# Down stage of a hybrid decoder trunk: where activations' high parts, the plain fills' reads, the last block's sums and the norm pieces stand in each engine's order

## The reference

```python
def hybrid_layer(x, p_i, ...):                  # x: 1 x 1024 tokens x 1024
    ...                                         # token mixing, not touched
    h = rmsnorm(x, norm_ffn)
    gu = h @ w_gate_up
    x = x + (jax.nn.silu(gu[..., :D_FF]) * gu[..., D_FF:]) @ w_down    # D_FF = 2816
    hp = rmsnorm(x, norm_ple)
    x = x + jax.nn.sigmoid(hp @ w_ple_gate) * (p_i @ w_ple_proj)
    return x

def reference(...):
    for i in range(DEPTH):                      # DEPTH = 2
        x = hybrid_layer(x, p[i], ...)
    return rmsnorm(x, norm_final)
```

## Time and profile before

| | us |
|---|---|
| median of 3 runs | 2526.24 |
| the 3 runs | 2511.62, 2527.43, 2526.24 |
| the profiled execution | 2511.84 |
| its span, first to last instruction | 2510.1 |
| PE busy | 2432.6 (97%) |
| DVE, ACT, POOL busy | 1538.7, 968.4, 1207.7 |
| mean granted clock of TensorE | 0.991 of full speed |

### The profile page before, as it was taken

One profiled execution on the slowest core, in us unless ns is written; L12 is line 12 of the kernel. 1 busy time (PEld: TensorE's weight loads), 2 busy tenths in 40 slices (PEclk: granted clock), 3 DMA queues, 4 the chain that ended last, 5 costly groups with the idle time before them and its releaser, 6 DMA issues. The chain is left out here.

```text
span 2510.1 us, 30190 instructions
## 1 busy us (share of the span) xinstructions
PE 2432.6 (97%) x11528; PEld 2000.1 (80%) x11528; DVE 1538.7 (61%) x1946; ACT 968.4 (39%) x1424; POOL 1207.7 (48%) x772
## 2 busy tenths in 40 slices
PE   7999999999999989899999999999999999989898
PEld 6888888888888877777878887888888888777776
DVE  7967855554554566575596778546544544856735
ACT  4324244433333334345333242334333333333453
POOL 3212112288878847772221121123888787577520
PEclk9999999999999999999999999999999999999999
DMA  4342222123333354322143322311332334435111
GB/s 165 103 97 68 73 82 81 59 82 99 105 98 112 105 180 143 125 93 68 38 154 98 78 60 61 101 59 59 99 115 84 114 107 137 167 113 164 51 46 72
DMA packets 108415, 245.92 MB, mean 98 GB/s; under 512 B 35688, under 2 KB 44136, under 8 KB 104432
## 3 DMA queue, kind: packets, MB, share of 16 engines
q1 hardware_dynamic: 60880, 126.90, 16.6%
q10 hardware_dynamic: 47392, 117.09, 13.8%
HBM read 179.43 MB, written 51.41 MB: 92 GB/s over the span
## 5 line engine op out<-in xcount | busy, mean ns | idle before, releaser
L2116 POOL TENSOR_TENSOR w_lo<-w_raw,w_hi 128x1024 fp32r<-128x1024 f32 x100 | 261.1, 2611 | 922.6 <-ACT w_hi L1556 922.4
L2164 PE MATMUL proj<-h_hi,w_hi 128*128 128x512 f32 x1376 | 545.4, 396 | 0.9 <-POOL w_lo L2116 0.9
L2166 PE MATMUL proj<-h_lo,w_hi 128*128 128x512 f32 x1376 | 536.1, 390 | 0.0
L2165 PE MATMUL proj<-h_hi,w_lo 128*128 128x512 f32 x1376 | 535.7, 389 | 0.0
L2123 POOL TENSOR_TENSOR w_lo<-w_raw,w_hi 128x512 fp32r<-128x512 f32 x180 | 261.2, 1452 | 181.5 <-ACT w_hi L1538 181.5
L2164 PEld LDWEIGHTS proj<-h_hi,w_hi 128*128 128x128 f32 x1376 | 258.4, 188 | 57.3 <-issue 3.1
L2166 PEld LDWEIGHTS proj<-h_lo,w_hi 128*128 128x128 f32 x1376 | 258.3, 188 | 54.4
L2165 PEld LDWEIGHTS proj<-h_hi,w_lo 128*128 128x128 f32 x1376 | 258.4, 188 | 53.7 <-issue 2.4
L2123 POOL TENSOR_TENSOR w_lo<-turns,w_hi 128x512 fp32r<-128x512 f32 x180 | 253.9, 1411 | 98.0 <-ACT w_hi L1538 97.9
L1538 ACT ACTIVATE w_hi<-w_raw 128x512 fp32r<-128x512 f32 x180 | 112.6, 629 | 296.7 <-PE aux L2228 92.9
L1538 ACT ACTIVATE w_hi<-turns 128x512 fp32r<-128x512 f32 x180 | 113.5, 630 | 248.9 <-PE proj L2228 99.1
(11 more groups left out here) (329 smaller groups left out, 5295.8 us busy)
## 6 DMA issues: line engine op xcount, KB each, us to landing
w_raw<-weights SPq DMA_DIRECT2D x160, 512.0 KB, 3.5
turns<-weights SPq DMA_DIRECT2D x60, 512.0 KB, 4.0
act_sums_spill<-rows ACTq DMA_DIRECT2D x20, 1024.0 KB, 6.8
h_whole<-act_sums_spill ACTq DMA_DIRECT2D x40, 512.0 KB, 4.1
act_sums_spill<-act ACTq DMA_DIRECT2D x20, 512.0 KB, 5.2
ffn_b_whole<-act_sums_spill ACTq DMA_DIRECT2D x20, 512.0 KB, 4.9
act_sums_spill<-act ACTq DMA_DIRECT2D x20, 256.0 KB, 4.4
ffn_bw_whole<-act_sums_spill ACTq DMA_DIRECT2D x10, 512.0 KB, 3.6
```

What stands on the lines that cost most here:

```text
L2116: g.tensor_tensor(wlo[:, slot, 0:n], w, whi[:, slot, 0:n].bitcast(F32), ALU.subtract).then_inc(weights_ready.sem, 1)
L2164: pe.matmul(out, wh, rhi, start=first, stop=False)
L2165: pe.matmul(out, wl, rhi, start=False, stop=False)
L2166: return pe.matmul(out, wh, rlo, start=False, stop=final)
```

## The change

Four orders are written differently; no arithmetic is added or removed.
1. On ACT, in the groups: `load_part` and `act_high` now stand ahead of `highs_ahead`.
2. On DVE, in the plain fills: the fills' adds come first, and the last block's two `finish_act` and its three sums stand between them; low parts 5 and 6 move into group 0.
3. On ACT, ahead of and in the plain fills: the first high part ahead of the last store of activations, the store of the sums behind the weight operands.
4. The norm's pieces: fewer of them in groups 8 and 9, 8 of the 16 squares move behind group 9 (ACT: between the reads of the projection's fills), and PE's `sums` from behind fill 9 to behind fill 15.

```diff
@@ vector
                     v.wait_ge(up_scaled.sem, up_scaled.at(L, 2 * b + 2))
-                    finish_act(L, NSTD + b, 1)
-                    finish_act(L, NSTD + b, 0)
-                    act_sums(L, b)
+                    if b < NBS - 1:
+                        finish_act(L, NSTD + b, 1)
+                        finish_act(L, NSTD + b, 0)
+                        act_sums(L, b)
@@ vector, ffn_down
                 for k in range(16):
                     add_fill(L, U_DN + k // 8, k % 8, k // 2, k % 2)
-                    if k % 2 and k < 14:
-                        act_low(L, NSTD + k // 2)
+                    if k in (0, 1):
+                        finish_act(L, FT - 1, 1 - k)
+                    if k in (3, 5, 7):
+                        if k == 3:
+                            for h in range(2):
+                                v.wait_ge(act_made.sem, act_made.at(L, 2 * FT))
+                        act_sum(L, 2 * DPARTS - 1, (k - 1) // 2)
+                    if k in (4, 6, 9, 11, 13):
+                        act_low(L, NSTD + (4, 6, 9, 11, 13).index(k))
...
                         down_add(L, g, i)
+                        if g == 0 and i in (0, 1):
+                            act_low(L, NSTD + 5 + i)
...
                         elif g == NDB - 1:
-                            if i == 0:
-                                ple_square(L, 5)
-                                ple_square(L, 6)
-                            if i == 1:
-                                ple_square(L, 7)
-                            if i == 2:
-                                ple_lows(L, 0, 2)
-                            if i == 3:
-                                ple_square(L, 8)
-                                ple_square(L, 9)
-                                ple_lows(L, 2, 4)
-                            if i == 4:
-                                ple_lows(L, 4, 6)
-                            if i == 5:
-                                ple_square(L, 10)
-                                ple_square(L, 11)
-                                ple_lows(L, 6, 7)
-                for j in range(12, 16):
+                            if i in (0, 1):
+                                ple_square(L, 4 + 2 * i)
+                                ple_square(L, 5 + 2 * i)
+                            elif i < 6:
+                                ple_lows(L, i - 2, i - 1)
+                ple_lows(L, 4, 16)
+                for j in range(8, 16):
                     ple_square(L, j)
-                ple_lows(L, 7, 16)
@@ scalar, ffn_down
-                store_block(L, NBS - 1)
-                for i in range(3):
+                act_high(L, NSTD)
+                store_acts(L, NBS - 1)
+                for i in (1, 2):
                     act_high(L, NSTD + i)
                 a.wait_ge(unit_done.sem, unit_done.at(L, U_DN + 1))
                 highs_ahead(L, 7 * NBS + 2)
                 highs_ahead(L, 7 * NBS + 3)
+                store_sums(L, NBS - 1)
                 for i in range(3, 7):
                     act_high(L, NSTD + i)
...
                         a.wait_ge(product_done.sem, product_done.at(L, k + 1))
-                        highs_ahead(L, k + 6)
                         if q < DPARTS - 1:
                             if not second:
                                 load_part(L, q + 1, i)
                             if (i >= 4) == (not second):
                                 act_high(L, NSTD + 7 * (q + 1) + (i + 3 if second else i - 4))
-                        elif not second:
+                        highs_ahead(L, k + 6)
...
@@ scalar, ple_proj
                             if k < 4:
                                 ple_early(L, 12 + k, 13 + k)
+                            elif k < 12:
+                                ple_square(L, 4 + k)
@@ tensor, ple_proj
-                            if k == 9:
+                            if k == 15:
                                 sums(L, 16, 2, early=14)
```

More of the change, by code:

```diff
@@ L1081, in act_sums, with act_sum @@
                     return
[L1082 to L1086, removed]
+                for k in (1, 2, 3):
+                    act_sum(L, p, k)
+            def act_sum(L, p, k):
+                t = [t_four(j) for j in range(4)]
+                if k == 1:
+                    v.wait_ge(act_summed.sem, act_summed.at(L, 4 * p + 1))
+                    v.tensor_tensor(t[1], act_t[:, 1, 0, :], t[0], ALU.add).then_inc(act_summed.sem, 1)
+                if k == 2:
+                    v.wait_ge(act_summed.sem, act_summed.at(L, 4 * p + 2))
+                    v.tensor_tensor(t[2], t[1], act_t[:, 0, 1, :], ALU.subtract).then_inc(act_summed.sem, 1)
+                if k == 3:
+                    v.tensor_tensor(t[3], act_t[:, 1, 1, :], t[1], ALU.subtract).then_inc(act_summed.sem, 1)
             def plain_gate(L, f):
@@ L1586, in store_block, with store_sums @@
                     a.dma_start(sums_d[:, p, 0, :], act_t[:, 0, 1, :]).then_inc(even_stored.sem, 16)
[L1587 to L1588 removed]
+                else:
+                    a.dma_start(sums_d[:, p, 1:3, :], act_t[:, 1, :, :]).then_inc(odd_stored.sem, 16)
+            def store_sums(L, b):
+                p = b // 2
                 a.wait_ge(act_summed.sem, act_summed.at(L, 4 * p + 4))
@@ L1719, in ffn_down @@
                                 act_high(L, NSTD + 7 * (q + 1) + (i + 3 if second else i - 4))
-                        elif not second:
+                        highs_ahead(L, k + 6)
+                        if q == DPARTS - 1 and not second:
                             if i == 0:
@@ L1727, in ffn_down @@
                                     a.activation(phi[w], p_whole[w], ACT.Copy).then_inc(p_hi_made.sem, 1)
[L1728 to L1733, removed]
+                            if i in (5, 6):
+                                ple_square(L, 2 * (i - 5))
+                                ple_square(L, 2 * (i - 5) + 1)
+                        elif q == DPARTS - 1:
                             for u in range(U_PROJ, U_PROJ + RING):
@@ L1736, in ffn_down @@
                                     units_high(L, u)
[L1737 to L1757, removed]
+                            if i in (0, 1):
+                                ple_square(L, 4 + 2 * i)
+                                ple_square(L, 5 + 2 * i)
+                            first, last = ((0, 0), (0, 4), (4, 5), (5, 6), (6, 8), (8, 10), (10, 12))[i]
+                            ple_early(L, first, last)
                 if L < DEPTH - 1:
```

13 lines of the change are left out of this document (8 added, 5 removed).

## The result

| | median | all runs | granted clock |
|---|---|---|---|
| before | 2526.84 us | 2511.62 to 2527.68 (4) | 0.991 in the profiled run |
| after | 2445.14 us | 2444.64 to 2445.41 (4) | 0.998 in the profiled run |

The ratio is 0.9686 (95% interval 0.9653 to 0.9719): 3.1% faster. The forecast was 2452 us, from 2438 to 2477. The profiled execution of after took 2445.41 us, 66.4 us less than that of before; the forecast's sum was 66.3.

A forecast was written before the change was run, and what follows sets the result against it. PE was taken as the bound, busy 97%, with stalls and lower clock to gain. Terms 36.8 + 15.8 + 11.7 + 2.0 = 66.3 us gave 2511.84 - 66.3 = 2445.5; plus 7 of offset, 2452 us, range 2438 to 2477.

The forecast's parts named there:

- What bounds the kernel: PE busy 97%; waits and lower clock in both layers' plain fills and ten groups make 65.8 us, 2.6% of the run.
- Part 1: Odd groups 1, 3, 5, 7: high parts ahead of weights' on ACT remove eight stalls at product 6, 36.8 us.
- Part 2: Plain fills: adds ahead of most finishes and sums on DVE remove PE's stall, 15.8 us over both layers, clock included.
- The tie at fills 11 to 15: Plain fills: DVE and PE tie from fill 11 on; 0.5 us of stall kept in each layer, bounds 0 and 2.
- the upper end: Plain fills: DVE and GpSimd locking each other out each time makes adds' upper end times hold, 1 us later in each layer.
- Part 3: Group 9 and projection: moving norm pieces gains 11.7 us in the groups and 2.0 at ACT's projection wait.
- Sum: Whole kernel: 36.8 + 15.8 + 11.7 + 2.0 = 66.3 us, 2445.5 against the profiled execution; likeliest median 2452.
- The offset: Median of before 14.4 us above its profiled execution: 6.4 may go with the stalls, 8 may stay; cases 2460 or 2445.
- DVE as the bound: Rival, plain fills and group 9: contended DVE prices hold throughout, giving 2476 us; chance 0.13, in full or half.
- POOL as the bound: Rival, groups: POOL's 11-instruction chain takes 25.3 us in place of 19.04, giving 2573 us; chance 0.03.

The follow-up runs named there:

- the swap on DVE alone: Kernel before with ACT unchanged; only DVE's low part 6 moved behind `down_add` 4 in the odd groups: 2478.09 us, ratio 0.9822.
- part 1 alone: Kernel before with only ACT's loads and activations' high parts moved ahead of the weight operand in the groups: 2474.23 us, ratio 0.9813.
- run without part 1: Kernel after with ACT's old order in the groups restored: 2492.81 us, ratio 0.9883 to the kernel before.

## Why the prediction was right, point by point

- **What bounds the kernel**: right. Two stretches a layer and the projection held the gain; after, PE is busy in 99% of the span.
- **Part 1**, by its chain: right, and shown from both ends. The swap on ACT alone removed eight stalls, and so did the swap on DVE alone. Its size was 36.8 us against before's profiled run, and the profiled execution of part 1 alone is 37.9 shorter. By the medians it was too small: added to before it gave 52.4 us (2526.66, the runs of before beside it, less 2474.23); taken from after it cost 47.7. The term was sized for eight stalls of which four had the clock fall; in the profiled run without part 1 seven had, and the clock took 18.6 us beside 27.8 of waiting.
- **Part 2**: 15.8 us forecast, 15.8 by the stretches (7.86 + 7.92), 15.5 by the kernel without it. The tie at fills 11 to 15, for which I kept 0.5 us a layer, is there in the first layer, 0.75 us in and behind the gaps at fills 11 and 12, and not in the second (21.88 us, where 21.8 is PE's own pace). The working had a slip that happened to cost nothing: add 6 at 2149.1 has the second sum at 0.7 us, while the price stated for a sum was 1.6, and by that adds 6 to 8 end some 0.9 us later, and PE stands at fill 11 even at the lower prices of what follows. Measured, that sum took 1.19 us in the first layer and 0.68 in the second. What I hadn't priced is the 1.2 us more ahead of the second layer's fills. The rule of the Trainium skill (SBUF — State Buffer, "SBUF: two separate sides"), by which the later of a DVE instruction with two SBUF inputs and a GpSimd instruction that reads SBUF waits for the whole of the other, fits the prices in the fills: low parts 0 and 1 took 1.72 and 1.71 us in the first layer, 1.73 and 1.21 in the second, where 1.21 is the shortest. With the `finish_act` that waited 1.01 us for ACT, these made the first layer's adds late. So something near the upper end, 1 us, came in one layer of two.
- **Part 3**: 11.7 + 2.0 forecast; 49.1 us over the 20 groups against 48.5 for parts 1 and 3 together, and 66.5 - 15.8 - 49.1 + 1.2 = 2.8 us left for the two projections against 2.0; 15.1 by the kernel without it. PE's wait at the projection is gone in both layers. Each projection is 1.8 us shorter; the second matmul of the gate then follows the first after 0.63 us in place of 0.23, which takes back 0.4.
- **Sum**: 66.3 forecast against the profiled run, 66.4 measured. That it fits to 0.1 us is luck: the groups gave 0.6 and the projections 0.8 more than their terms, and 1.2 went ahead of the fills. By the medians the gain is 81.7 us, of which the parts taken out one at a time make 47.7 + 15.5 + 15.1 = 78.3.
- **The offset**: the step that was mis-sized. I let half of the 14.4 us between before's profiled run and its median stay, since only 4 x 1.6 = 6.4 of it could be clock behind the stalls. None stayed, and 2445.5 instead of 2452 would have been the number. The price of 1.6 us was too low: in the run without part 1 the clock behind a stall of the same length cost 6.2 - 3.8 = 2.4 us in four groups. Eight stalls at 6.2 us would be 49.6, 13 us above the 36.8 of before's profiled run (an estimate from these rows), so they can account for nearly all of the offset. The runs of before agree: their clocks fall as their times rise, 0.991 to 0.981, and most of the spread goes with the eight stalls. A trace of one of the long runs of before isn't on record, so it is not shown that all of the 14.4 us is clock. The sentence of the Trainium skill (TensorE: Matmul & The Clock Gate, "What's actually happening") on a phase that differs from run to run pointed to 2445; the runs agree in that the mean clock of one kernel differed from run to run, and what sets it was not seen.
- **Rivals**: DVE as the bound didn't come; the adds kept pace but for those 0.75 us. POOL as the bound is real as a mechanism, and its work was 17.0 us a group, as in the odd groups before (17.2). It begins to cost at 18.8 (6.2 us lost) and costs 56.2 at 21.3, where the kernel is still 0.8% faster than before. The 22.7 us from which I said it would turn the result lie beyond that, and no run reached them.

## What to carry to other kernels

On engines that work in order, look at what stands *behind* a waiting instruction, on its own engine and on the next one: the wait that PE showed was two queues away from the sum that caused it, and either queue could be reordered to cure it. A list of waits names the last link only; when a link named is cured and the time doesn't move, add up the work of each engine per round before reordering again. Price a stall by its idle time and by the longer busy time of the same matmuls, and look at the clock of several runs before calling an offset a constant.

## What the runs showed of the hardware

- Eight stalls of 3.5 us, one in each of groups 1, 3, 5 and 7 of both layers, cost 27.8 us of idle time and 18.6 of lower clock; a single one took 3.8, 5.4 or 6.2 us in all. The mean clock differed from run to run of one program: 2511.8 us at 0.991, 2530.2 at 0.981. In the kernel after, without them, it was 0.998 in all four runs.
- The same low part on DVE (128x1024) took from 1.21 to 2.68 us in the kernel after, an add that reads PSUM 1.21 to 1.22 wherever the lines above show it; a 128x512 low part on POOL took 1.28 to 2.30. One more instruction of 1.3 us on POOL lengthened its group by 1.8 (17.0 to 18.8).
